# Moving three groups of work and folding one more projection chunk in a one-layer hybrid mixer with a mixture of experts

## The chip, the core and the metric

The kernel runs on one core of one Trainium2 chip. The metric is the device time of one execution in microseconds. The engines of the core are TensorE (PE, with its weight loads as PEld), VectorE (DVE), ScalarE (ACT), GpSimd (POOL) and SyncE (SP); 16 DMA engines move data between DRAM and the on-chip memory. Everything is float32.

## What is computed

272 tokens (16 learned meta tokens and 256 of the sequence) of width 2048 pass one decoder layer. The normalised tokens go through one input projection into 52 tiles of 128 columns; an HGRN, an mLSTM and a Mamba-2 mixer read them; the joined outputs go through an output projection and are added to the residual. A mixture of 32 experts follows (one group, then two experts in it, for each token), with a residual add and a last norm. In short:

```python
h = concat([meta, x])                                   # 272 x 2048
u = rmsnorm(h, norm_mix_w)
proj = u @ w_in                                         # 2048 x ~6.7k
(hq, hf, hi, hg, mq, mk, mv, mo, mi, mf, sz, sxbc, sdt) = split_last(proj, IN_SPLITS)
y_a = hgrn2_mixer(hq, hf, hi, hg, lower_bounds, hg_norm_w)
y_b = mlstm_mixer(mq, mk, mv, mo, mi, mf, ml_b_i, ml_b_f, ml_norm_w)
y_c = mamba2_mixer(sz, sxbc, sdt, conv_w, conv_b, dt_bias, a_log, d, ssm_norm_w)
h = h + concat([y_a, y_b, y_c]) @ w_out                 # 2048 x 2048
h = h + hierarchical_moe(rmsnorm(h, norm_ffn_w), ...)   # 32 experts, 3 matrices of 4 MB each
return rmsnorm(h, final_norm_w)[:, N_META:]

# where it matters below
f = lower_bound + (1 - lower_bound) * sigmoid(hf)       # HGRN's decay; its log is summed over the tokens
y_b = group_rmsnorm(h_ml, norm_w, 4) * sigmoid(mo)      # mo: the last four tiles, MO
y_c = group_rmsnorm(y * silu(z), norm_w, 4)
```

## The kernel before, in words

Each engine has its own instruction stream, written out by hand; the order of the work is the order in those streams, and semaphores tie them together. Nothing is planned by a program.

**Projections.** The input projection is worked through in 26 chunks (c = 0 to 25) of 256 columns, two tiles of 128 columns each (u = 2c and 2c + 1), in the order of `ORDER`: HF, HQ, HV, X0, B0, C0, MQ, MK, MV, HG_, Z0, MO. Chunks 2 and 3 are HQ, chunks 4 and 5 HV, chunk 19 is the second half of HG_, chunks 20 to 23 are Z0, and chunks 24 and 25 the four MO tiles. Eight more chunks (26 to 33) are the output projection. A chunk of weights is 2 MB. SP loads it (L506) into one of two buffers as soon as TensorE has finished the chunk two places before (`in_tile`, L498). ACT takes a finished tile out of PSUM (`tile_out`, L793).

**Folded chunks.** For the chunks in `FOLD` (L228) the product of a chunk is not made as 2 x 16 products over all tokens, but by a seven-product scheme on 2 x 2 blocks: `folded_tiles` makes blocks 0 to 6, each of 8 products over half of the tokens. Blocks 2, 4 and 6 (and 3) need sums and differences of weight blocks, made on POOL by `weight_sums(c)` in four instructions (L643, L645, L646, L650), where block 2 waits for the second, block 3 for the third and block 6 for the fourth. The sums of a folded chunk after the first start when block 4 of the folded chunk before is done (`fold_ps`). The matching sums of token blocks, `uS`, are made once on DVE by `sums_of_tokens` (L1163 to L1168); they are written over hT, the residual, so the residual is first written to DRAM (`h_rows`, L490), and DVE waits for that write (`X_IN[0]`). After the last folded chunk SP loads it back (L500). DVE joins the blocks with `adds_a` and `adds_b` (L1174); block 5 waits for the first of these additions.

**The start.** SP loads the tokens, chunks 0 and 1 and three narrow strips `wg`, and then writes `h_rows` (L489, L490, waiting for ACT's ninth copy `x_ev`). ACT issues ten small parameter loads (L773). TensorE makes the first tiles, the gate products (L1945), then turns the parameters (L1753, waiting for all ten loads), and goes on with tiles 2 to 7.

**HGRN's part around chunk 4.** DVE makes a memset (L1354), the token sums, and then eight scalings (L1358, L1360) which end in the signal `hlin`; ACT makes the logarithm (L882) and only then takes out tiles 6 and 7; DVE scales HQ (L1364), makes four scans (L1368), four differences (L1242, L1243) and then the additions of chunk 4. Block 2 of chunk 4 waits for tile 7's being taken out.

**Mamba's part around chunk 19.** DVE makes for eight pairs of heads the decays (`ssm_decay`, L1291) and the scores (`ssm_scores`, L1302, six instructions, signal `pt_ready`). TensorE's `ssm_pair` (L1911) waits for them. POOL, having spread the last rows, starts the sums of chunk 19 when its weights have landed.

**The end of the mixers.** Chunk 24 is not folded. ACT takes out its tiles with a sigmoid (L942, L945), squares what the norms need and makes the inverse roots (`inverse_rms`); TensorE makes the norms' sums (L1894) behind tiles 49 and 50.

**The experts.** From expert 0 on SP streams the 96 matrices of 4 MB through four buffers, each load released by TensorE's having used the one before it in its buffer.

Of the kernel before, what the change touches and what calls it, by code (L numbers as in the profile page):

```python
# [28 lines left out]
def hymba_moe_layer(nc, x, meta_tokens, hg_lb_logits, norm_mix_w, w_in, hg_norm_w, ml_b_i, ml_b_f,  # L29
# [7 lines left out]
    ACT = mybir.ActivationFunctionType  # L37
# [5 lines left out]
    NM = meta_tokens.shape[0]  # L43
    SEQ = x.shape[1]
    T = NM + SEQ
    KD = D // P
# [4 lines left out]
    HGH, MLH, SSH, SSG = 4, ml_b_i.shape[1], ssm_d.shape[1], 4  # L51
# [47 lines left out]
    with ctx:  # L99
# [17 lines left out]
        def wchunk(j):  # L117
            return slot(j).rearrange("p (k c) -> p k c", k=KD)
# [108 lines left out]
        wT = part(13376, NA * P)  # L227
        FOLD = (4, 5, 11, 12, 13, 19, 20, 21, 22, 23)  # L228
        NF = len(FOLD)
# [241 lines left out]
        def columns(w, c):  # L471
            return w[0, :, bass.ds(c, CH)].rearrange("(k p) c -> p k c", p=P)

        @block.sync
        def _(sp):
# [12 lines left out]

            sp.wait_ge(s["x_ev"], 9)  # L489
            sp.dma_start(h_rows, big[:, RING + KD * T:RING + 2 * KD * T]).then_inc(X_IN[0], 16)  # L490
            for c in range(2, (NIN + NOUT) // 2):
# [6 lines left out]
                sp.wait_ge(s["in_tile"], 2 * c - 2)  # L498
                if c == FOLD[-1] + 2:
                    sp.dma_start(big[:, RING + KD * T:RING + 2 * KD * T], h_rows).then_inc(X_IN[1], 16)  # L500
                w, col = (w_in, COLS[2 * c]) if 2 * c < NIN else (w_out, P * (2 * c - NIN))
                if 2 * c == NIN + NOUT - 2:
                    for h in range(2):
                        sp.dma_start(last_chunk[:, h, :, :], columns(w, col)[:, :, h * P:(h + 1) * P]).then_inc(s["in_b"], 16)
                else:
                    sp.dma_start(wchunk(c % 2), columns(w, col)).then_inc((s["in_a"], s["in_b"])[c % 2], 16)  # L506
                if 2 * c == NIN + 2:
                    sp.wait_ge(s["norm_done"], 1)
                    sp.dma_start(eslot(0), matrix(0, 0)).then_inc(m_in[0], 16)
# [58 lines left out]
        def _(pool):  # L568
# [61 lines left out]
            def weight_blocks(c):  # L630
                w = wchunk(c % 2)
                return [[w[:, 8 * k:8 * (k + 1), j * P:(j + 1) * P] for j in range(2)] for k in range(2)]

            def weight_sums(c):
                n = FOLD.index(c)
                s1, s2, s4 = sums_at(c)
                (b11, b12), (b21, b22) = weight_blocks(c)
                if c == 13:
                    pool.wait_ge(s["ho_ps"], HGH)
                if n:  # L640
                    pool.wait_ge(s["fold_ps"], 5 * n)
# [85 lines left out]
        def _(act):  # L727
# [198 lines left out]
            for u in range(40, 48):  # L926
# [11 lines left out]
                if u == 47:  # L938
                    act.wait_ge(s["in_ev"], 4 + 48)
                    V.activation(proj[:, Z0 + 4:Z0 + 8, :], proj[:, Z0 + 4:Z0 + 8, :], ACT.Silu).then_inc(s["z_gate"], 1)  # L940
                    den_abs(3)
            tile_out(48, ACT.Sigmoid)  # L942
            squares(s["ml_h"], MLH, mlo, sqH)
            act.dma_start(nwc[:, :], norm_ffn_w[0].rearrange("(p c) -> p c", c=KD)).then_inc(s["nw_in"], 16)
            tile_out(49, ACT.Sigmoid)  # L945
            squares(s["ssm_gated"], 1, proj[:, Z0:Z0 + 8, :].rearrange("p (g j) t -> p j g t", j=2),
                    sq8.rearrange("p (j g) t -> p j g t", j=2))
            inverse_rms(1, 1, rs4)
            tile_out(50, ACT.Sigmoid)
            inverse_rms(2, 2, rs4z)  # L950
# [117 lines left out]
        def _(dve):  # L1068
# [389 lines left out]
            for c in range(4, 8):  # L1458
                last = V.tensor_tensor(proj[:, Z0 + c, :], proj[:, Z0 + c, :], proj[:, X0 + c, :], ALU.mult)
            last.then_inc(s["ssm_gated"], 1)  # L1460
            step.link(group_norm(1, mlo, rs4, 4, 1, PL))
            group_norm(2, proj[:, Z0:Z0 + 8, :], rs4z, 4, 2, PS).then_inc(s["z_done"], 1)
            dve.wait_ge(s["in_ev"], 4 + NIN)
            for h in range(MLH):
# [884 lines left out]
```

## Time and profile before

| | |
|---|---|
| median of 3 runs | 1493.99 us (1492.85 to 1494.16) |
| profiled execution | 1492.35 us, of which the span is 1490.4 us |
| PE busy | 1266.8 us (85%) |
| DVE busy | 529.2 us (36%) |
| ACT busy | 279.5 us (19%) |
| POOL busy | 179.6 us (12%) |
| DMA engines, first 14 of 40 slices | 2 to 9 tenths busy |
| DMA engines, last 24 slices | 9 tenths or more, about 430 GB/s |
| PEclk, first 16 slices | 9 tenths or more |
| PEclk, later | 8 or 9 tenths |

The span is cut into 40 slices of 37.3 us. The projections and mixers fill the first 15 of them; the rest is the experts. A time like 339.89 is counted from the start of the span. The page's chain of work that ended last gives PE 52% and DMA 43% of the span.

### The profile page before, as it was taken

The page shows a single profiled execution, that of the slowest core. Times are in us where ns is not written, and L with a number is a line of the kernel's source. Part 1 is how long each engine was busy: PE and PEld are TensorE (multiplying, and loading weights), DVE is VectorE, ACT ScalarE, POOL GpSimd, SP SyncE. Part 2 cuts the span into 40 slices and gives each one's busy share as a digit, 9 for nine tenths or more (in the row PEclk, how much of TensorE's full clock was granted, in tenths as well). Part 3 has the DMA queues.
Part 4 walks back from the last instruction along what each step waited for, and adds up shares of the span by engine and source line. Part 5 has one row for each costly group of instructions (what it writes and reads, how often), then busy time and mean ns, then how long its engine had stood idle before and what let it go on. Part 6 is the DMA issues. An engine that isn't in the chain of part 4 may idle for free.

```text
span 1490.4 us, 20152 instructions
## 1 busy us (share of the span) xinstructions
PE 1266.8 (85%) x8506; PEld 757.1 (51%) x8506; DVE 529.2 (36%) x1177; ACT 279.5 (19%) x423; POOL 179.6 (12%) x144
## 2 busy tenths in 40 slices
PE   8999999999999999876878688778768776787797
PEld 6898899778999995322222232223222322232242
DVE  3543666444624214452232223223322321322234
ACT  3212413112240123111111111111111110000003
POOL 3140043015604730000000000000000000000000
PEclk9999999999999999989898888888898988888898
DMA  9442354444557668999999999999999999999997
GB/s 294 155 151 85 104 141 150 144 135 125 159 173 260 249 206 358 433 429 431 431 430 430 433 432 431 433 432 431 432 433 433 428 432 434 427 431 433 428 432 316
DMA packets 107051, 488.88 MB, mean 328 GB/s; under 512 B 20012, under 2 KB 91976, under 8 KB 93288
## 3 DMA queue, kind: packets, MB, share of 16 engines
q1 hardware_dynamic: 104608, 483.11, 80.5%
q0 software_dynamic: 1104, 3.49, 0.7%
q10 hardware_dynamic: 1272, 1.28, 0.2%
q8 instruction: 54, 0.88, 0.2%
q14 instruction: 13, 0.11, 0.0%
HBM read 483.40 MB, written 4.61 MB: 327 GB/s over the span
## 4 chain that ended last, share of the span: by engine, by line
PE 52%; DMA 43%; DVE 3%; issue 1%; ACT 0%; ACTq 0%; SPq 0%; POOL 0%; DVEq 0%; POOLq 0%
DMA big<-in_moe_w_dram 41%; PE bank L1719 22%; PE bank L2156 8%; PE bank L2078 5%; PE bank L2185 3%; PE bank L2198 3%; PE bank L1832 2%; PE bank L2132 2%; PE bank L2169 2%; PE bank L1869 1%; PE bank L1845 1%; DVE big L1302 1%; PE bank L1911 1%; DMA brow<-in_moe_b_router_dram 1%; DMA out_dram<-big 1%
## 5 line engine op out<-in xcount | busy, mean ns | idle before, releaser
L2156 PE MATMUL bank<-big 128*32 128x512 f32 x2016 | 292.0, 733 | 192.4 <-DMA big<-in_moe_w_dram 191.3
L1719 PE MATMUL bank<-big 128*128 128x272 f32 (+4 forms) x2144 | 365.6, 331 | 2.5 <-ACT big L793 1.3
L1719 PEld LDWEIGHTS bank<-big 128*128 128x128 f32 x2144 | 320.2, 191 | 37.8 <-ACT big L793 1.9
L2156 PEld LDWEIGHTS bank<-big 128*32 128x32 f32 x2016 | 74.2, 131 | 406.3 <-issue 207.3
L1558 DVE COPY big<-bank 128x512 f32<-128x512 f32 x32 | 22.1, 691 | 510.5 <-PE bank L2156 509.7
L1571 DVE TENSOR_TENSOR big<-big,bank 128x512 f32<-128x512 f32 x240 | 146.1, 679 | 12.3 <-PE bank L2198 12.3
L2185 PE MATMUL bank<-big 128*32 128x512 f32 x992 | 127.8, 661 | 0.5 <-DVE big L1563 0.5
L2198 PE MATMUL bank<-big 32*128 32x512 f32 x480 | 127.1, 633 | 0.7 <-ACT big L1020 0.7
L721 POOL DMA_INDIRECT out_dram<-big,mlev x1 | 1.1, 1089 | 812.1 <-DMA out_dram<-big 812.1
L1007 ACT ACTIVATE big<-bank 128x512 f32<-128x512 f32 x32 | 19.1, 597 | 369.8 <-PE bank L2132 369.8
L2198 PEld LDWEIGHTS bank<-big 32*128 32x128 f32 x480 | 46.8, 183 | 61.8 <-DVE big L1571 41.2
L2185 PEld LDWEIGHTS bank<-big 128*32 128x32 f32 x992 | 31.6, 119 | 91.2 <-issue 90.2
L2078 PE MATMUL bank<-big 128*128 128x128 f32 x672 | 76.7, 276 | 0.0
L2078 PEld LDWEIGHTS bank<-big 128*128 128x128 f32 x672 | 75.7, 192 | 0.1
L2169 PEld LDWEIGHTS bank<-selq,big 128*128 128x128 f32 x496 | 57.7, 191 | 26.0 <-issue 26.0
L2132 PE MATMUL bank<-big 128*32 128x512 f32 x512 | 62.3, 607 | 6.6 <-issue 6.6
L1020 ACT ACTIVATE big<-bank 128x512 f32<-128x512 f32 x31 | 18.5, 597 | 252.5 <-PE bank L2185 252.5
L2169 PE MATMUL bank<-selq,big 128*128 128x32 f32 x496 | 61.1, 277 | 0.0
L643 POOL TENSOR_TENSOR big<-big 128x1024 f32<-128x1024 f32 x10 | 24.0, 2401 | 164.6 <-DMA big<-in_w_in_dram 109.6
L1495 DVE TENSOR_TENSOR big<-big,bank 128x256 f32<-128x256 f32 (+1 forms) x54 | 18.4, 360 | 64.2 <-PE bank L2078 64.2
L1011 ACT ACTIVATE big<-bank 128x512 f32<-128x512 f32 x32 | 19.1, 597 | 116.9 <-PE bank L2156 116.9
L793 ACT ACTIVATE big<-bank 128x272 f32<-128x272 f32 (+1 forms) x30 | 12.2, 410 | 150.8 <-PE bank L1719 150.8
(345 smaller groups left out, 1098.2 us busy)
## 6 DMA issues: line engine op xcount, KB each, us to landing
big<-in_moe_w_dram SPq DMA_DIRECT2D x92, 4096.0 KB, 32.7
big<-in_w_in_dram SPq DMA_DIRECT2D x25, 2048.0 KB, 8.3
big<-in_w_out_dram SPq DMA_DIRECT2D x7, 2048.0 KB, 8.4
big<-in_moe_w_dram SPq DMA_DIRECT2D x6, 2048.0 KB, 21.0
big<-in_moe_w_dram SPq DMA_DIRECT2D x4, 1024.0 KB, 20.2
h_rows<-big SPq DMA_DIRECT2D x1, 2176.0 KB, 8.8
big<-gate_rows POOLq DMA_DIRECT2D x8, 272.0 KB, 3.6
big<-h_rows SPq DMA_DIRECT2D x1, 2176.0 KB, 9.0
```

What stands on the lines that cost most here:

```text
L643: V.tensor_tensor(s1, b12, b11, ALU.subtract).then_inc(s["fold_ready"], 1)
L1007: V.activation(xs, pb[0][:, :], ACT.Copy).then_inc(signal("xs_ev", x), 1)
L1558: V.tensor_copy(hs3.rearrange("t (k p) -> t k p", p=P), pb[3][:, :].rearrange("t (p k) -> t k p", k=KF)).then_inc(signal("h3_ev", x), 1)
L1571: V.tensor_tensor(h2[:, a, d * 512:(d + 1) * 512], h2[:, a, d * 512:(d + 1) * 512], pb[SUM_BANKS[j]][:, :], ALU.add).then_inc(signal("y_ac ...
L1719: last = V.matmul(outs, a, b, start=start and j == 0, stop=stop and j == n - 1)
L1832: last = V.matmul(pb[(OUT0 + u % 2) % 4][:, 0:SEQ], w, proj[:, MIXED[k], NM:T], start=k == 0, stop=k == 7)
L2078: last = V.matmul(pb[(7 * n + i + 2 + OUT0) % 4][:, 0:SH], w[:, k, :], m, start=k == 0, stop=k == 7)
L2132: last = V.matmul(pb[0][CAP * g:CAP * (g + 1), :], oh[:, a, :], u2[:, a, g * 512:(g + 1) * 512], start=a == 0, stop=a == NA - 1)
L2156: last = V.matmul(pb[2 + r][CAP * g:CAP * (g + 1), :], xsT[:, k % 4, k // 4, :], w[:, k, :], start=j == 0, stop=j == 3)
L2169: last = V.matmul(pb[4][:, (r * KF + k) * CAP:(r * KF + k + 1) * CAP], hs[:, k * P:(k + 1) * P], selq[:, :], start=True, stop=True)
L2185: last = V.matmul(pb[5][CAP * g:CAP * (g + 1), :], hTb[:, k * CAP:(k + 1) * CAP], w[:, k, g * 512:(g + 1) * 512], start=k == 0, stop=k == ...
L2198: V.matmul(pb[SUM_BANKS[j]][:, :], wT[CAP * g:CAP * (g + 1), a * P:(a + 1) * P], ysb[CAP * g:CAP * (g + 1), :], start=True, stop=True).the ...
```

## The change

There are four parts.

1. The write of the residual to `h_rows` and its wait move from ahead of the loop over the chunks to behind the load of chunk 3.
2. Two waits are added on POOL: the sums of chunk 4 wait for `hlin` (HGRN's eight scalings), and those of chunk 19 for the eighth `pt_ready` (the last scores).
3. Chunk 24 is folded too. TensorE makes it in seven blocks; POOL makes four sums more; DVE's additions for it stand ahead of the group norms; ACT copies its first block, and makes the sigmoid of both tiles in one instruction behind the first inverse roots, and DVE waits for that (`z_gate`). With one folded chunk more, the PSUM banks of the chunks behind it turn by one.
4. The load of the residual back from `h_rows` is issued one chunk later (26 in place of 25), and behind that chunk's weights in place of ahead of them.

```diff
-        FOLD = (4, 5, 11, 12, 13, 19, 20, 21, 22, 23)
+        FOLD = (4, 5, 11, 12, 13, 19, 20, 21, 22, 23, 24)
...
-            sp.wait_ge(s["x_ev"], 9)
-            sp.dma_start(h_rows, big[:, RING + KD * T:RING + 2 * KD * T]).then_inc(X_IN[0], 16)
             for c in range(2, (NIN + NOUT) // 2):
...
                 sp.wait_ge(s["in_tile"], 2 * c - 2)
-                if c == FOLD[-1] + 2:
-                    sp.dma_start(big[:, RING + KD * T:RING + 2 * KD * T], h_rows).then_inc(X_IN[1], 16)
...
                     sp.dma_start(wchunk(c % 2), columns(w, col)).then_inc((s["in_a"], s["in_b"])[c % 2], 16)
+                if c == FOLD[-1] + 2:
+                    sp.dma_start(big[:, RING + KD * T:RING + 2 * KD * T], h_rows).then_inc(X_IN[1], 16)
+                if c == 3:
+                    sp.wait_ge(s["x_ev"], 9)
+                    sp.dma_start(h_rows, big[:, RING + KD * T:RING + 2 * KD * T]).then_inc(X_IN[0], 16)
...
                 (b11, b12), (b21, b22) = weight_blocks(c)
+                if c == 4:
+                    pool.wait_ge(s["hlin"], 1)
                 if c == 13:
                     pool.wait_ge(s["ho_ps"], HGH)
+                if c == 19:
+                    pool.wait_ge(s["pt_ready"], SSH // 2)
...
-            tile_out(48, ACT.Sigmoid)
+            first_product(24)
             squares(s["ml_h"], MLH, mlo, sqH)
             act.dma_start(nwc[:, :], norm_ffn_w[0].rearrange("(p c) -> p c", c=KD)).then_inc(s["nw_in"], 16)
-            tile_out(49, ACT.Sigmoid)
             squares(s["ssm_gated"], 1, proj[:, Z0:Z0 + 8, :].rearrange("p (g j) t -> p j g t", j=2),
                     sq8.rearrange("p (j g) t -> p j g t", j=2))
             inverse_rms(1, 1, rs4)
+            act.wait_ge(s["in_ev"], 4 + 50)
+            V.activation(proj[:, MO:MO + 2, NM:T], proj[:, MO:MO + 2, NM:T], ACT.Sigmoid).then_inc(s["z_gate"], 1)
             tile_out(50, ACT.Sigmoid)
...
             last.then_inc(s["ssm_gated"], 1)
+            adds_a(24)
+            adds_b(24)
             step.link(group_norm(1, mlo, rs4, 4, 1, PL))
             group_norm(2, proj[:, Z0:Z0 + 8, :], rs4z, 4, 2, PS).then_inc(s["z_done"], 1)
+            dve.wait_ge(s["z_gate"], 3)
             dve.wait_ge(s["in_ev"], 4 + NIN)
```

## Rows read from the trace of the kernel before

**Rows 1.** Busy time by stretch: start, length, PE, PEld, DVE, ACT, POOL, PEclk, DMA, GB/s
```profile
620.00:900.00 280.00, 215.65 (x1444) 77.58 (x1448) 85.15 (x194) 43.86 (x57) 3.16 (x10) 0.87 1.00 431
```

**Rows 2.** Waits behind 560: waiting line, what it waited for, total us, times, longest
```profile
PE bank L2156 <- DMA big<-in_moe_w_dram: 191.3, 55, 7.4
```

**Rows 3.** Timeline of SP at 578: start, length, engine, line, operation, tensors, count
```profile
578.00 0.33 SPq L525 DMA_DIRECT2D big<-in_moe_w_dram  x1
```

**Rows 4.** Timeline of PE, start to 90; in brackets the idle time before and its releaser
```profile
32.88 0.33 PE L1753 MATMUL bank<-ident,big 128*128 128x128 f32 x1 [2.41 <-DMA brow<-in_moe_b_router_dram]
...
63.85 17.79 PE L1719 MATMUL bank<-big 128*128 128x256 f32 x96 [0.50 <-DVE colc L1156]
82.95 5.83 PE L1719 MATMUL bank<-big 128*128 128x136 f32 x48 [1.31 <-ACT big L793]
89.34 10.92 PE L1719 MATMUL bank<-big 128*128 128x136 f32 x92 [0.56 <-DVE big L1174]
```

**Rows 5.** Timeline of PE, around the last pair and around chunks 23 and 24
```profile
339.89 1.14 PE L1911 MATMUL bank<-big 128*64 128x272 f32 x12 [2.35 <-DVE big L1302]
...
405.47 12.77 PE L1719 MATMUL bank<-big 128*128 128x128 f32 x112
...
420.41 14.08 PE L1719 MATMUL bank<-big 128*128 128x256 f32 x64
```

**Rows 6.** SP's issues of the residual's write and of chunk 3; the page's DMA issue row
```profile
23.09 0.96 SPq L490 DMA_DIRECT2D h_rows<-big  x1
...
49.03 0.37 SPq L506 DMA_DIRECT2D big<-in_w_in_dram  x1
...
h_rows<-big SPq DMA_DIRECT2D x1, 2176.0 KB, 8.8
```

**Rows 7.** DMA queues (packets, MB, share): SP's q1 and ACT's q10, 26:27; q10, 30:31
```profile
q1 hardware_dynamic: 23, 0.40, 93.4%
q10 hardware_dynamic: 23, 0.00, 1.6%
...
q10 hardware_dynamic: 330, 0.02, 21.4%
```

**Rows 8.** Timeline of DVE, 64 to 89
```profile
64.22 1.50 DVE L1354 MEMSET big<- 128x1728 f32 x1 [0.43 <-DVE colc L1156]
...
71.51 0.41 DVE L1360 TENSOR_SCALAR big<-big,lb 128x272 f32<-128x272 f32 x1
71.84 2.45 DVE L1358 TENSOR_SCALAR big<-big,lb 128x272 f32<-128x272 f32 x1
...
83.21 0.73 DVE L1364 TENSOR_SCALAR big<-big 128x1088 f32<-128x1088 f32 x1 [1.74 <-ACT big L793]
83.85 2.56 DVE L1368 TENSOR_TENSOR_SCAN big<-ones,big 128x272 f32<-128x272 f32 x4
...
89.00 1.50 DVE L1174 TENSOR_TENSOR big<-big,bank 128x136 f32<-128x136 f32 x5
```

**Rows 9.** Timeline of ACT, the logarithm
```profile
81.51 1.11 ACT L882 ACTIVATE big<-big 128x1088 f32<-128x1088 f32 x1 [16.96 <-DVE big L1360]
```

**Rows 10.** Timeline of POOL: first sums of chunks 4, 5, 19 and 23
```profile
71.77 2.36 POOL L643 TENSOR_TENSOR big<-big 128x1024 f32<-128x1024 f32 x1 [10.94 <-DMA big<-in_w_in_dram]
...
88.86 2.44 POOL L643 TENSOR_TENSOR big<-big 128x1024 f32<-128x1024 f32 x1 [7.55 <-PE bank L1719]
...
329.64 2.35 POOL L643 TENSOR_TENSOR big<-big 128x1024 f32<-128x1024 f32 x1 [2.92 <-DMA big<-in_w_in_dram]
...
398.56 2.36 POOL L643 TENSOR_TENSOR big<-big 128x1024 f32<-128x1024 f32 x1 [6.42 <-PE bank L1719]
```

**Rows 11.** Timeline of DVE: scores of pairs 6 and 7; second half of the Z products
```profile
322.72 1.75 DVE L1302 SCALAR_TENSOR_TENSOR big<-big,colc 128x272 f32<-128x272 f32 x6
...
330.89 8.94 DVE L1302 SCALAR_TENSOR_TENSOR big<-big,colc 128x272 f32<-128x272 f32 x6
...
423.74 1.49 DVE L1459 TENSOR_TENSOR big<-big 128x272 f32<-128x272 f32 x4
```

## The prediction

> **What bounds the kernel now.** I read the busy times by stretch first. In the experts' part the DMA engines are busy throughout (1.00, 431 GB/s) while PE is busy 215.65 of 280 us [rows 1], and PE's greatest wait there is for the weights, 191.3 us [rows 2]. So that part lasts as long as its bytes, whatever TensorE does. What matters is when it begins: from 578.00 on every load is released by TensorE's having used a buffer [rows 3], and that moment is the end of the mixers and the output projection, where PE is busy nearly throughout. So the second view is PE's timeline up to there, read for its gaps. A microsecond of PE idle taken away ahead of 578 should start the stream a microsecond earlier and be a microsecond off the end. The gaps that the change can reach are four: 2.41 us ahead of the parameters' transposes, 1.31 and 0.56 us in chunk 4 [rows 4], 2.35 us ahead of the last pair of heads [rows 5]. Besides them it shortens a busy stretch, chunk 24.
>
> **Part 1, the residual's write.** PE waits for the parameters 2.41 us, until 32.88 [rows 4]. SP issued the write of 2.2 MB at 23.09, and it landed 8.8 us later [rows 6], so it was on the way until 31.9. Between 26 and 27 SP's queue moved 23 packets with 0.40 MB, 17 KB each, and ACT's queue, which carries the parameters, moved 23 too, all tiny. The two queues took turns, packet by packet, and a tiny packet waited out a large one each time. Between 30 and 31, when the write was through, ACT's queue moved 330 [rows 7]. Without the write its backlog needs some 2 us: five microseconds at 25 a microsecond and the 330 make about 450 packets, which at 330 a microsecond are gone by about 27. With 2 us for landing that is 29, and PE is ready at 32.88 - 2.41 = 30.47. The gap goes entirely: **-2.4 us**. Bounds: 0 and 2.41, since PE has work right up to it.
> The Trainium skill says the same of the queues (DMA: Bandwidth & Descriptors, Queues, rings and completion order: each DMA engine goes round its queues and changes at packet boundaries). By that rule the write disturbs whoever shares the engines with it, now POOL's loads of the gate rows; what this can do stands in the rivals.
>
> Where does the write go? All times of before up to chunk 4 move 2.4 earlier. Chunk 3 is issued at 49.03 - 2.4 = 46.6 [rows 6]; nothing else of SP waits behind the write for long (chunk 4 is issued when tile 5 is done, some 14 us later; `x_ev` is long there). The 2 MB of chunk 3 go ahead of it at about 0.4 MB a microsecond [rows 7], 5.3 us, then the write's 8.8: it lands at about 61.1 with 1 us for the issues counted in. DVE needs it for the token sums, behind the memset: 64.22 + 1.5 - 2.4 = 63.3 [rows 8]. The slack is 2 us; at the cost of nothing, then, as long as the write takes under 11 us from chunk 3's end.
>
> **Part 2a, the sums of chunk 4.** DVE's scalings took 0.33 us each (71.51 to 71.84) until POOL began at 71.77 [rows 10], then 2.45 [rows 8]: each waited for one POOL instruction. The last four cost 8 us more, the logarithm started at 81.51 [rows 9], and tiles 6 and 7 came out behind it: PE's 1.31 us. DVE came to the additions at 89.00 [rows 8]: PE's 0.56 us. With the wait, DVE makes eight scalings in 8 x 0.33 from 70.5 - 2.4 on: `hlin` at 70.8. POOL's four sums follow, 9.5 us, until 80.4. ACT: logarithm until 72, tile 6, then tile 7 when PE has it. PE: 63.85 + 17.79 - 2.4 = 79.2 is when block 2 is wanted, and the two blocks before it take 5.83 / 3 = 1.94 each, so tile 7 is ready at 75.3 and out at 75.75. The second sum, which block 2 needs, is there at 70.8 + 4.8 = 75.6. So the 1.31 us go. Block 5 is wanted at 79.2 + 5.83 = 85.1, and the first addition must be done. DVE has from the scaling of HQ to the additions 89.00 - 83.21 = 5.8 us of work [rows 8], but now POOL runs beside it from 75.75 to 80.4. The HQ scaling ends with POOL's third instruction, about 78. The scans (two inputs in SBUF) have no row beside POOL. Their price is bounded by 0.65 each (2.56 for four [rows 8]) and by one POOL instruction, 2.4, for each that meets one. I take the dear end, since the scores with the same operand kinds pay it [rows 11]: one scan until 80.5, then three scans and four differences, 4.5 us, additions at 85.0, first one done at 85.3. PE waits 0.2, against 0.56 before; with cheap scans nothing. The gain is 1.87 - 0.2: **-1.7 us**, bounds 1.9 and, by the rival below, -0.8 (a loss).
> The Trainium skill (SBUF — State Buffer, SBUF: two separate sides) has the rule: VectorE and GpSimd share a port pair as an exclusive lock, for a fast-mode VectorE operation or one with two inputs in SBUF. By it the scans are blocked as I took them; were the lock for fast modes alone, the 0.2 us would be nothing. The six scores of part 2b, which have two such inputs, took 8.94 in place of 1.75 us, so the trace agrees.
>
> **Part 2b, the sums of chunk 19.** Pair 6's scores took 1.75 us, pair 7's 8.94 from 330.89 on, while POOL's sums ran from 329.64 [rows 10, 11]; PE waited 2.35 for them [rows 5]. PE wants the scores at 337.5. Uncontended they are done at 332.6, 5 us ahead. POOL starts there, 3 us later than before, and has its second sum at 337.4, its fourth at 342.2. PE makes the pair 337.5 to 338.6 and blocks 0 and 1 until 342.2; block 2 finds its sum 5 us old, block 6, another 7 us on, its own as well. What is queued behind POOL's wait are only these sums; the last row loads stand ahead of it. **-2.35 us**, bounds 2.35 and 2.35 less one POOL instruction.
>
> **Part 3, chunk 24 folded.** Unfolded it takes 14.08 us, folded chunk 23 of the same width 12.77 [rows 5]: **-1.3 us**. Its sums start when block 4 of chunk 23 is done, 405.47 + 5 x 1.8 = 414.6, and end at 424.1; block 2 is wanted at 420.4 + 3.6 = 424.0, block 6 at 431. For chunk 23 POOL began 6.9 us ahead of the chunk [rows 5, 10], here 5.8. DVE's last products were at 423.74 to 425.2 [rows 11]; now one or two of its operations wait for POOL, 2.4 at most beyond 424.1: additions from 426 or 427 on, wanted at 429.5. ACT's one sigmoid over two tiles is bounded by the 1.11 us of an instruction with twice the elements [rows 9], plus a table load, and lies beside tile 50's 7 us. POOL's pair sum of squares waits behind the sums, and has 10 us. Part 4, the residual's load back, leaves with chunk 26's weights: two transfers of 5.3 us from about 433 on, done by 447, and DVE wants it at 464. Neither PE nor the stream sees it. Bounds of part 3: 1.3 and 1.3 - 2.4 (one more blocked operation than the slack holds).
>
> **The sum.** 2.4 + 1.7 + 2.35 + 1.3 = 7.75 us of PE time ahead of 578, all on the path. The profiled execution took 1492.35 (span 1490.4): 1484.6, span 1482.7. Its time lies 1.6 under the median of the runs, 1493.99, whose scatter is 1.3: forecast **1486.3**.
>
> **The rivals.**
> - *One blocked difference in chunk 4.* POOL's sums for chunk 5 start at 85.15, when block 4 is done (88.86 after 88.78 before [rows 4, 10]). DVE's last difference starts at 84.35. If DVE is some 0.8 us later it meets POOL and ends at 87.5: PE waits 2.7 us. The time is 1486.3 + 2.5 = 1488.8. For it: the write shares the engines with some 1.4 MB of gate rows; byte for byte shared, it would land 3 us later, over its slack by 1. Against: [rows 7] show turns by packet, in which 2 KB packets hold up 17 KB ones little. Chance 0.13.
> - *The parameters are no earlier*, because their own issue or latency, not the write, held them: 1488.7. Against it stand the 330 packets of one microsecond [rows 7]. Chance 0.05.
> - *The stream doesn't start earlier* or gives the gain back, being bound by its bytes: 1493.5 or so. Against: up to 578.00 the loads wait for PE [rows 3]. Chance 0.05.
> - *Slower: DVE is caught in POOL's chunk 5 sums altogether.* With five or more two-input operations left at 85.15 it gets one step for each of POOL's four sums and then finishes, 96 us: PE waits 11 us in chunk 4, and 1.87 + 2.4 + 2.35 + 1.3 = 7.9 are not enough: 1493.99 - 7.9 + 11 = 1497.1. It decides from a landing of the write at 66 or later, 5 us beyond my estimate. Chance 0.02.
>
> **How the numbers follow.** Forecast 0.70, the four rivals 0.25, the rest (small shifts of either sign) 0.05. A measurement of this kernel can tell 0.2%, 3 us, from no change. Faster by more: 0.70 + 0.13 + 0.05 and most of the rest, 0.92; same 0.05, slower 0.03. The range takes in the forecast, the first two rivals and the scatter of 0.7 to either side: 1484.5 to 1489.8.
>
> **What would show it.** The row of L1753 has no idle time before it and starts near 30.5. The write is issued near 47 and DVE's token sums start near 63. All eight scalings take 0.41. L643 of chunk 4 follows `hlin`; PE's gap before block 2 is gone, the one before block 5 at most 0.3. The eighth L1302 group takes 1.75, and PE's gap before L1911 is gone. Chunk 24 stands as 112 instructions of 12.8 us. The first buffer's reload, 578.00 before, is at about 570.3. Wrong would be: DVE idle ahead of its token sums for the write, a difference (L1242, L1243) of 2.4 us, or a stream that starts earlier and ends no earlier.

## The result and the profile after

The change makes the kernel **slower**: 1498.44 us (median of 8 runs, 1497.78 to 1499.6) against 1494.0 for the kernel before (median of 8, 1492.85 to 1494.98); the ratio is 1.0021, with a 95% interval of 1.0012 to 1.0031. The forecast was 1486.3, its range 1484.5 to 1489.8. The profiled execution took 1497.94, its span 1496.2.

Three of the four gains did arrive, 6.0 us together, but more is lost at two other places. First TensorE's gaps in the mixers (timeline of PE, kernel after: start, length, line, operation, tensors, count, and in brackets the idle time before and its releaser):

```profile
30.58 0.33 PE L1762 MATMUL bank<-ident,big 128*128 128x128 f32 x1
...
61.56 19.95 PE L1728 MATMUL bank<-big 128*128 128x256 f32 x112 [0.50 <-DVE colc L1162]
82.15 3.94 PE L1728 MATMUL bank<-big 128*128 128x136 f32 x32 [0.64 <-POOL big L651]
95.30 14.89 PE L1728 MATMUL bank<-big 128*128 128x136 f32 x113 [9.20 <-DVE big L1180]
...
336.78 1.14 PE L1920 MATMUL bank<-big 128*64 128x272 f32 x12
...
344.95 1.14 PE L1920 MATMUL bank<-big 128*64 128x272 f32 x12
...
425.49 12.77 PE L1728 MATMUL bank<-big 128*128 128x128 f32 x112
...
455.36 13.98 PE L1841 MATMUL bank<-big 128*128 128x256 f32 x64
```

The parameters' transposes start at 30.58 with no idle time, 2.3 us earlier than before [rows 4]. The last pair has lost its gap [rows 5], and chunk 24 takes 12.77 in place of 14.08. But ahead of block 5 of chunk 4 TensorE now waits 9.20 us, where it waited 0.56. What this does to the lead over the kernel before: chunk 4 begins 2.29 us earlier (61.56 against 63.85), the seventh pair 7.49 later (336.78 against 329.29), the eighth 5.06 later, the output projection's 64 products 3.76 later (455.36 against 451.60). The experts' stream starts as much later (SP, kernel after; against 578.00 in [rows 3]):

```profile
581.77 0.33 SPq L526 DMA_DIRECT2D big<-in_moe_w_dram  x1
```

The engines that feed block 5, DVE first (kernel after):

```profile
63.34 1.23 DVE L1169 TENSOR_TENSOR big<-big 128x1088 f32<-128x1088 f32 x1
...
70.55 0.41 DVE L1366 TENSOR_SCALAR big<-big,lb 128x272 f32<-128x272 f32 x1
76.11 0.94 DVE L1370 TENSOR_SCALAR big<-big 128x1088 f32<-128x1088 f32 x1 [5.16 <-ACT big L798]
76.98 8.96 DVE L1374 TENSOR_TENSOR_SCAN big<-ones,big 128x272 f32<-128x272 f32 x4
85.97 0.73 DVE L1248 TENSOR_TENSOR big<-big 128x544 f32<-128x544 f32 x1
86.61 2.87 DVE L1249 TENSOR_TENSOR big<-big 128x544 f32<-128x544 f32 x1
89.40 2.86 DVE L1248 TENSOR_TENSOR big<-big 128x544 f32<-128x544 f32 x1
92.18 2.86 DVE L1249 TENSOR_TENSOR big<-big 128x544 f32<-128x544 f32 x1
94.96 1.50 DVE L1180 TENSOR_TENSOR big<-big,bank 128x136 f32<-128x136 f32 x5
```

and POOL (kernel after):

```profile
52.80 0.74 POOL L622 DMA_DIRECT2D gate_rows<-gX  x1 [22.92 <-DVE gZ L1159]
...
61.41 0.58 POOL L628 DMA_DIRECT2D big<-gate_rows  x1 [6.84 <-DMA gate_rows<-gZ]
62.22 1.61 POOL L628 DMA_DIRECT2D big<-gate_rows  x3 [0.22 <-issue]
74.12 2.36 POOL L648 TENSOR_TENSOR big<-big 128x1024 f32<-128x1024 f32 x1 [10.28 <-DMA big<-in_w_in_dram]
76.56 2.71 POOL L650 TENSOR_TENSOR big<-big 128x1024 f32<-128x1024 f32 x1
79.23 2.77 POOL L651 TENSOR_TENSOR big<-big 128x1024 f32<-128x1024 f32 x1
81.97 2.77 POOL L655 TENSOR_TENSOR big<-big 128x1024 f32<-128x1024 f32 x1
86.17 2.72 POOL L648 TENSOR_TENSOR big<-big 128x1024 f32<-128x1024 f32 x1 [1.44 <-PE bank L1728]
```

DVE is on time: its token sums start at 63.34, its eight scalings end at 70.96, as forecast. POOL isn't. Its sums start at 74.12, and what released them is **chunk 4's weights**, not `hlin`, 3.2 us earlier. From 76.98 to 84.7 and again from 86.17 on each of DVE's two-input operations then takes as long as a POOL instruction: three of the four scans 2.8 to 2.9 us each, while the fourth, behind POOL's last sum, takes 0.69 (8.96 together, 2.56 before [rows 8]), and three differences 2.9 each in place of 0.72. So the additions stand at 94.96 and not at 85.0.

Why the weights are late stands in the DMA issues (kernel after, the stretches 47 to 50, 50 to 56 and 60 to 61: operation and count, KB each, us from issue to landing):

```profile
h_rows<-big SPq DMA_DIRECT2D x1, 2176.0 KB, 13.8
...
gate_rows<-gX POOLq DMA_DIRECT2D x1, 17.0 KB, 6.7
gate_rows<-gG POOLq DMA_DIRECT2D x1, 4.2 KB, 6.9
gate_rows<-gZ POOLq DMA_DIRECT2D x1, 4.2 KB, 7.1
...
big<-in_w_in_dram SPq DMA_DIRECT2D x1, 2048.0 KB, 13.4
```

The write is issued at 47.15 and lands at 61.0. POOL's three tiny writes of gate rows, issued in that time, took 2.3, 1.9 and 1.8 us before and take 6.7 to 7.1 now. POOL waits for them [6.84 <-DMA gate_rows<-gZ] and reads the rows back at 61.41 instead of 58.43, which is 2.3 us earlier plus a 5.3 us delay. By then chunk 4's load (issued at 60.55) is under way, and the two share the engines: between 66 and 70 POOL's queue moved 0.97 MB and SP's 0.31. Chunk 4's weights take 13.4 us where they took 8.9.

On top of this TensorE's **granted clock** falls (kernel after: start, length, busy time of PE, PEld, DVE, ACT, POOL, then PEclk, DMA share and GB/s):

```profile
88.00:90.00 2.00, 0.00 (x0) 0.00 (x0) 2.00 (x2) 0.00 (x0) 1.92 (x2) 0.56 0.00 0
...
96.00:98.00 2.00, 2.00 (x11) 2.00 (x11) 0.46 (x2) 0.00 (x0) 0.00 (x0) 0.50 0.00 0
98.00:100.00 2.00, 2.00 (x17) 2.00 (x17) 0.30 (x1) 0.00 (x0) 0.00 (x0) 0.88 0.04 8
100.00:102.00 2.00, 2.00 (x19) 2.00 (x19) 0.30 (x1) 0.00 (x0) 1.12 (x1) 1.00 0.09 6
```

0.50 is 1.2 GHz: TensorE makes 11 products in 2 us in place of 19 or 20, until some 3 us after it has work again. From 95.3 on, 2.7 us at 0.50 and 2 at 0.88 cost 1.6 us. The sum up to the seventh pair: 10.06 us of gaps in chunk 4 (9.20, 0.64, and 0.22 within the row of 19.95, whose products took 17.79 and 1.94 before) against 1.87 are 8.2 more, the clock 1.6, the start was 2.3 earlier: 7.5, and 7.49 is read.

The second place is the **tail**. Of the span's 5.8 us more, 3.77 are there at the stream's start and 3.15 at DVE's last instruction; then POOL is another 2.67 late with the last rows of the output. Kernel after:

```profile
1487.16 0.75 DVE L1718 SCALAR_TENSOR_TENSOR big<-big,mlev 128x512 f32<-128x512 f32 x1
1491.87 1.09 POOL L726 DMA_INDIRECT out_dram<-big,mlev  x1 [813.36 <-issue]
```

and kernel before:

```profile
1484.01 0.75 DVE L1709 SCALAR_TENSOR_TENSOR big<-big,mlev 128x512 f32<-128x512 f32 x1
1486.05 1.09 POOL L721 DMA_INDIRECT out_dram<-big,mlev  x1 [812.06 <-DMA out_dram<-big]
```

Before, POOL starts 2.04 us behind the start of DVE's last product, released by an output write; after, 4.71 us behind, and waiting for nothing that the profile shows. In between lies one packet of an instruction queue (q14, between 1489 and 1490); before, it comes only after POOL's write is issued (between 1491 and 1492).

### The profile page after: what moved, and what is told of

It is laid out like the page before. It is cut to its first block, busy times and chain, and to the rows that moved or that the text cites. A ratio compares the mean times of both kernels' runs of the same rounds, so it can differ in the third digit from the quotient of the medians.

```text
span 1496.2 us, 20269 instructions
## 1 busy us (share of the span) xinstructions
PE 1275.5 (85%) x8554; PEld 760.3 (51%) x8554; DVE 529.9 (35%) x1184; ACT 279.0 (19%) x422; POOL 190.7 (13%) x148
## 3 DMA queue, kind: packets, MB, share of 16 engines
q0 software_dynamic: 1104, 3.49, 0.7%
## 4 chain that ended last, share of the span: by engine, by line
PE 56%; DMA 41%; DVE 2%; issue 1%; ACT 0%; SPq 0%; POOL 0%; DVEq 0%; POOLq 0%
DMA big<-in_moe_w_dram 40%; PE bank L1728 24%; PE bank L2165 8%; PE bank L2087 5%; PE bank L2194 4%; PE bank L2207 3%; PE bank L1841 2%; PE bank L2141 2%; PE bank L2178 2%; PE bank L1878 1%; PE bank L1854 1%; DVE big L1374 1%; PE bank L1920 1%; DMA big<-in_x_dram 1%; DMA out_dram<-big 0%
## 5 line engine op out<-in xcount | busy, mean ns | idle before, releaser
L2165 PE MATMUL bank<-big 128*32 128x512 f32 x2016 | 292.9, 735 | 187.7 <-DMA big<-in_moe_w_dram 186.6
L1728 PE MATMUL bank<-big 128*128 128x128 f32 (+4 forms) x2192 | 366.0, 327 | 10.5 <-DVE big L1180 9.2
L2194 PE MATMUL bank<-big 128*32 128x512 f32 x992 | 134.4, 690 | 0.5 <-DVE big L1572 0.5
L2141 PE MATMUL bank<-big 128*32 128x512 f32 x512 | 62.3, 607 | 3.3 <-DVE big L1547 3.3
L2178 PE MATMUL bank<-selq,big 128*128 128x32 f32 x496 | 61.1, 277 | 0.0
L1180 DVE TENSOR_TENSOR big<-big,bank 128x128 f32<-128x128 f32 (+2 forms) x77 | 20.8, 288 | 65.1 <-PE bank L1728 64.7
## 6 DMA issues: line engine op xcount, KB each, us to landing
big<-h_rows SPq DMA_DIRECT2D x1, 2176.0 KB, 14.2
```

What stands on the lines that cost most here:

```text
L1180: return V.tensor_tensor(out_, in_, pb[(START[c] + i) % 4][:, 0:m], ALU.add)
L1728: last = V.matmul(outs, a, b, start=start and j == 0, stop=stop and j == n - 1)
L2141: last = V.matmul(pb[0][CAP * g:CAP * (g + 1), :], oh[:, a, :], u2[:, a, g * 512:(g + 1) * 512], start=a == 0, stop=a == NA - 1)
L2165: last = V.matmul(pb[2 + r][CAP * g:CAP * (g + 1), :], xsT[:, k % 4, k // 4, :], w[:, k, :], start=j == 0, stop=j == 3)
L2178: last = V.matmul(pb[4][:, (r * KF + k) * CAP:(r * KF + k + 1) * CAP], hs[:, k * P:(k + 1) * P], selq[:, :], start=True, stop=True)
L2194: last = V.matmul(pb[5][CAP * g:CAP * (g + 1), :], hTb[:, k * CAP:(k + 1) * CAP], w[:, k, g * 512:(g + 1) * 512], start=k == 0, stop=k == ...
```

## The experiments

**The theory** from these traces: the write behind chunk 3 slows the small writes of gate rows, these put POOL's big reads into chunk 4's load, POOL starts its sums 3 us late, and DVE is caught with its scans in the sums of chunk 4 and with three differences in those of chunk 5. Rivals: the added wait for `hlin` does it; or the write itself, by its place in SP's queue; or the collision of DVE and POOL is no cause but a symptom.

**The write alone** (kernel before with part 1 only).

```diff
-            sp.wait_ge(s["x_ev"], 9)
-            sp.dma_start(h_rows, big[...]).then_inc(X_IN[0], 16)
...
+                if c == 3:
+                    sp.wait_ge(s["x_ev"], 9)
+                    sp.dma_start(h_rows, big[...]).then_inc(X_IN[0], 16)
```

> The kernel before with part 1 alone: the residual's write behind chunk 3, no wait added on POOL, chunk 24 unfolded. Theory (the write's new place): the write holds up POOL's three small row writes, which land near 61; the gate rows then run into chunk 4's load, its weights land near 74, and POOL's sums meet DVE's scans and differences although POOL has no wait. PE then idles about 9 us ahead of block 5 and its clock falls to 0.5 for a few us: 1494 - 2.3 + 8 + 1.5 = 1501 us. Rival (the added wait puts the sums on top of the scans): without that wait the gaps in chunk 4 stay near 2 us: 1491.5 us.

Measured: 1501.91 against 1494.99 on the same chip, ratio 1.0032 (1.0013 to 1.0051). Without any wait for `hlin` POOL's first sum stands where it does in the full change:

```profile
74.12 2.36 POOL L644 TENSOR_TENSOR big<-big 128x1024 f32<-128x1024 f32 x1 [10.50 <-DMA big<-in_w_in_dram]
```

The scans take 8.95, the last three differences 2.87, 2.86 and 2.86, TensorE waits 0.36, 0.64 and 9.20. With the write behind chunk 3 the added wait has no part in the loss of chunk 4; part 1 alone makes it. The loss is greater than the full change's because the gains of parts 2b and 3 are missing, and because in this execution the clock also stood at 0.50 behind the gap of 2.31 us ahead of the last pair: the stream starts at 587.08.

**The wait for `hlin` alone** (kernel before with part 2a only).

```diff
+                if c == 4:
+                    pool.wait_ge(s["hlin"], 1)
```

> The kernel before with the wait of chunk 4's sums on hlin alone. Theory (the write's new place is what hurts): hlin at 73.2, sums 73.2 to 83.5, HQ's scaling at 78.1 and one scan meet them, additions near 88, PE idle 0.5 to 1 us ahead of block 5 in place of 1.87 in two gaps; if the last difference meets chunk 5's sums, 3.5. 1493 us, 1495.5 at the worst. Rival (the wait itself): PE idle some 9 us ahead of block 5, 1501 us.

Measured: 1500.06 against 1494.99, 1.0033 (1.0021 to 1.0044), a miss for both. The sums follow `hlin`, and the scans take 4.72; but the last difference starts at 89.39, POOL's sums for chunk 5 at 89.06: it takes 2.86 us, and TensorE waits 3.54 us, after which the clock stands at 0.50 from 92 to 96. So part 2a costs more than it brings even where the write is at its old place: one gap of 3.54 us and the clock behind it, in place of 1.87 us in two gaps. Not all of the measured loss is its own. The clock fell two more times in this execution, behind gaps that the kernel before has too: the parameters' gap, here 2.75 us (0.76 and 0.50 from 32 to 36), and the last pair's, here 2.40 (0.76 and 0.50 from 346 to 350).

**The write behind chunk 2**, the rest of the change as it is.

```diff
-                if c == 3:
+                if c == 2:
```

> The changed kernel with the residual's write behind the load of chunk 2 in place of chunk 3, where no other transfer runs for some 10 us. Theory: parameters still early (PE gap of 2.4 gone), small row writes land in 2 us, chunk 4's weights near 70, POOL starts at hlin near 71. PE idle ahead of block 5 0.3 to 3: 1486.5 to 1489.5 us. Rival (the wait on hlin): chunk 4 stays as in the changed kernel, 1498 us.

Measured: 1491.46 against 1494.99, 0.9974 (0.9965 to 0.9984): faster than before, 2 us above the range expected. The small writes take 2.3, 1.9 and 2.0 us, chunk 4's load 8.7, and POOL starts behind `hlin` (timeline of POOL):

```profile
70.93 2.36 POOL L648 TENSOR_TENSOR big<-big 128x1024 f32<-128x1024 f32 x1 [12.30 <-DVE big L1366]
...
84.88 2.62 POOL L648 TENSOR_TENSOR big<-big 128x1024 f32<-128x1024 f32 x1 [4.04 <-PE bank L1728]
```

The loss left is the blocked difference, the first rival of the prediction (timelines of DVE and PE):

```profile
85.21 2.87 DVE L1249 TENSOR_TENSOR big<-big 128x544 f32<-128x544 f32 x1
...
88.34 21.99 PE L1728 MATMUL bank<-big 128*128 128x136 f32 x153 [3.54 <-DVE big L1180]
```

and the clock behind it is at 0.50 (busy time by stretch, columns as above):

```profile
90.00:92.00 2.00, 2.00 (x11) 2.00 (x10) 0.00 (x0) 0.00 (x0) 2.00 (x2) 0.50 0.00 0
```

**The write at its old place**, the rest of the change as it is.

```diff
+            sp.wait_ge(s["x_ev"], 9)
+            sp.dma_start(h_rows, big[...]).then_inc(X_IN[0], 16)
             for c in range(2, (NIN + NOUT) // 2):
...
-                if c == 3:
-                    sp.wait_ge(s["x_ev"], 9)
-                    sp.dma_start(h_rows, big[...]).then_inc(X_IN[0], 16)
```

> The changed kernel with the residual's write back at its old place, ahead of the loop. Theory: the parameters' gap of 2.4 us is back, chunk 4 as in the kernel with its wait alone, the pair's gap of 2.35 and 1.3 of chunk 24 are gone: 1489.5 us, up to 1492 if a difference meets chunk 5's sums. Rival (the wait on hlin): 1500 us.

Measured: 1496.56 against 1494.99, 1.0006 (0.9994 to 1.0018): a miss. The gap before block 5 is 3.55 us as in the two runs above, the parameters' gap 2.94, and the clock fell behind both. The stream starts at 580.99, 2.99 us later than before.

**The wait of chunk 19 alone** (kernel before with part 2b only).

```diff
+                if c == 19:
+                    pool.wait_ge(s["pt_ready"], SSH // 2)
```

> The kernel before with the wait of chunk 19's sums on the last scores alone. Theory (scores and sums exclude each other): pair 7's six scores take 1.75 us in place of 8.94, PE's gap of 2.35 ahead of them is gone, no new gap; the experts' first reload comes 2.35 earlier: 2.35 us less than before. Rival (part 2b gives nothing, since PE waits for the later sums instead): a gap of 2 us ahead of block 2 or 6 of chunk 19, same time as before.

Measured: 1490.59 against 1494.33, 0.9981 (0.9970 to 0.9993). The scores take 1.75 us, TensorE has no gap before the last pair. The stream starts at 574.75, 3.25 us earlier; of this some 0.9 is no work of the part, since chunk 4's gaps were 1.00 us in this execution against 1.87.

**Chunk 24's folding alone** (kernel before with parts 3 and 4):

```diff
-        FOLD = (4, 5, 11, 12, 13, 19, 20, 21, 22, 23)
+        FOLD = (4, 5, 11, 12, 13, 19, 20, 21, 22, 23, 24)
```

> The kernel before with parts 3 and 4 alone: chunk 24 folded, the residual's load back one chunk later. Theory: chunk 24 takes 12.8 in place of 14.1 us, no new gap up to 578, the experts' first reload 1.3 earlier: 1.3 us less than before. Rival (the rest of what was lost sits here, in the norms or the later load back): gap of PE between 434 and 470, or no earlier reload; same as before or 1 to 2 us more.

Measured: 1492.9 against 1494.33, 0.9992 (0.9979 to 1.0005), which can't be told from no change. Chunk 24 takes 12.77 us and there is no new gap, but the stream starts at 581.82, 3.8 us later than before, where 1.3 earlier was expected. Two falls of the clock did that, behind gaps which the kernel before has too: the parameters' gap was 2.94 us and the 32 products behind it took 10.53 in place of 7.60, and behind the last pair's gap TensorE makes 14 products in 2 us, where it made 21 at clock 1.00 (timeline of PE, then busy time by stretch):

```profile
343.47 1.80 PE L1915 MATMUL bank<-big 128*64 128x272 f32 x12 [2.31 <-DVE big L1303]
...
344.00:346.00 2.00, 2.00 (x14) 1.37 (x12) 0.50 (x1) 0.00 (x0) 0.00 (x0) 0.50 1.10 376
```

In TensorE's rows both parts do what the prediction says of them; that chunk 24's folding makes the whole kernel faster is not shown by these times.

**POOL's sums of chunk 5 held back** until DVE's differences are done, in the changed kernel, and **the same with the write behind chunk 2**. In the first, only the meeting of the differences with chunk 5's sums is taken away; the late weights and the held scans are left.

```diff
+                if c == 5:
+                    pool.wait_ge(s["lv_d"], 2)
```

> The changed kernel (write behind chunk 3) with POOL's sums of chunk 5 waiting for DVE's fourth difference. Theory: POOL still starts at 74.1 and the scans still take 9 us, but the differences take 0.7 each in place of 2.87, additions at 88.6, PE's gap ahead of block 5 falls from 9.2 to 2.9 us: 1492 us, some 1.5 to 3 more if the clock falls in a gap of this length. Rival (the differences are not held by POOL): gap stays at 9 us, 1498.4 us.

> The changed kernel with the write behind chunk 2, and POOL's sums of chunk 5 waiting for DVE's fourth difference. Theory (the last difference meets chunk 5's sums, and the idle time it makes costs the clock too): that difference takes 0.72 in place of 2.87 us, PE's gap ahead of block 5 falls from 3.5 to about 1.4 us, its clock stays at 1.00: 2.1 + 3 = 5 us less than with the write behind chunk 2 alone, 1486.5 us. Rival (idle time alone is lost, the clock costs nothing): 2.1 us less, 1489.4 us.

Measured: 1491.48 against 1494.87, 0.9972 (0.9958 to 0.9986), for the first, 1487.24 against 1494.33, 0.9956 (0.9943 to 0.9970), for the second. In the first POOL still starts at 74.25 and the scans still take 8.95, but the four differences take 0.72 each, the gap is 2.77 in place of 9.20, and the clock stays at 1.00. The stream starts at 573.92, 7.85 us earlier than in the changed kernel. So this collision is a cause: taking it away gives back 7 us, more than the whole loss. In the second the gap is 1.39 us, and the clock stays at 1.00 too.

**Chunk 4's fourth sum held back** in place of chunk 5's sums, with the write behind chunk 2. Block 6 alone needs that sum, so POOL may leave DVE alone during the scans. Chunk 5's sums follow it in POOL's stream, so they too come behind the differences.

```diff
-                if c == 3:
+                if c == 2:
...
+                if c == 4:
+                    pool.wait_ge(s["lv_d"], 2)
                 V.tensor_tensor(s4, b21, s2, ALU.subtract).then_inc(s["fold_ready"], 1)
```

> The changed kernel with the write behind chunk 2, and the fourth sum of chunk 4 (which only block 6 needs) waiting for DVE's fourth difference. Theory (each scan that meets POOL costs one POOL instruction): HQ's scaling meets the third sum, the scans nothing; additions near 83.5, where block 5 is wanted at 84.8: no gap in chunk 4, clock at 1.00, all that was forecast is there: 1485 us. Rival (block 6 waits for the late sum): a gap of 1 to 2 us one block later, 1487 us.

Measured: **1483.62** (1483.25 to 1484.06) against 1494.33, 0.9932 (0.9918 to 0.9946), the fastest of all. DVE, POOL and PE:

```profile
78.53 2.56 DVE L1376 TENSOR_TENSOR_SCAN big<-ones,big 128x272 f32<-128x272 f32 x4
...
83.83 2.37 POOL L657 TENSOR_TENSOR big<-big 128x1024 f32<-128x1024 f32 x1 [5.81 <-DVE big L1251]
...
61.42 47.36 PE L1730 MATMUL bank<-big 128*128 128x256 f32 x320 [0.50 <-DVE colc L1164]
...
569.43 0.33 SPq L526 DMA_DIRECT2D big<-in_moe_w_dram  x1
```

TensorE has no gap from the start of chunk 4 on through chunk 5, and the stream starts 8.57 us earlier than before.

**The clock's price.** Kernel: the write behind chunk 2, and in the gap before block 5 seven products of no use, so that TensorE isn't idle there.

```diff
+                    if c == 4:
+                        for _ in range(7):
+                            V.matmul(pb[7][:, 0:T], ones[:, 0:P], ones[:, :], start=True, stop=True)
```

> The changed kernel with the write behind chunk 2, and seven products of no use (ones by ones, into a free bank) on PE where it else idles 3.5 us ahead of block 5 of chunk 4. Theory (idle time lets the clock fall to 0.50 for six us, which costs 3 us of products): the products take 3.3 us, the granted clock stays at 1.00 from 84 to 96, block 5 starts at the same 88.3, and the time is 3 us less than with the write behind chunk 2 alone, 1488.5 us. Rival (the fall of the clock has another cause or costs nothing): 1491.5 us or more.

Measured: 1489.85 against 1494.87, 0.9964 (0.9951 to 0.9977). Block 5 starts at the same time, 88.29 in place of 88.34, but at clock 1.00:

```profile
90.00:92.00 2.00, 2.00 (x20) 2.00 (x19) 0.30 (x1) 0.00 (x0) 2.00 (x2) 1.00 0.00 0
```

The seventh pair starts at 328.24 against 331.27, and the stream 3.0 us earlier (573.23 against 576.25). So in these two executions the lower clock costs another 3.0 us behind a gap of 3.5. The medians differ by 1.6 only (1489.85 against 1491.46), where 3.0 was expected; the profiled execution without the filling, 1492.57, is the slowest of its ten (1490.05 to 1492.57), and whether the clock fell in the others isn't known. The Trainium skill says that TensorE falls to its lower clock behind idle time (TensorE: Matmul & The Clock Gate, Part 1). The traces agree in kind, but the length of the gap alone doesn't decide: of the parameters' gaps those of 2.75 and 2.94 us were followed by 0.50 and those of 2.41 and 2.72 were not; ahead of the last pair 2.31 and 2.40 were, 2.35 in the kernel before was not; ahead of block 5 every gap of 3.5 us or more was, and 2.77 was not.

**The gate rows read later**: the changed kernel, with POOL's four row reads placed behind chunk 4's sums.

```diff
+            weight_sums(4)
             for p in range(SSH // 2):
...
-                        if c <= 15:
+                        if 4 < c <= 15:
```

> The changed kernel (write behind chunk 3) with POOL's spreading of the first gate rows behind its sums of chunk 4. Theory (the write holds up the small row writes, so the gate rows' loads run into chunk 4's): chunk 4's load lands in 9 in place of 13.4 us, POOL starts at hlin near 71 in place of 74.1, chunk 4 then goes as with the write behind chunk 2, gap 3.5 us: 1491.5 us. Rival (the write itself delays chunk 4's load, being ahead of it in SP's queue): POOL starts near 74, gap 9 us, 1498 us.

Measured: 1491.57 against 1494.87, 0.9966 (0.9951 to 0.9980), as with the write behind chunk 2, and with a gap of 3.80 us before block 5. The write is still behind chunk 3 and the three small writes still take 6.8 to 7.0 us, but chunk 4's load takes 8.3, and POOL's first sum is released by `hlin`:

```profile
71.24 2.36 POOL L648 TENSOR_TENSOR big<-big 128x1024 f32<-128x1024 f32 x1 [16.88 <-DVE big L1367]
```

The weights were late because of the row reads, then, not because of the write's place in SP's queue.

**POOL's stream made longer**: the changed kernel with 40 tiny memsets in POOL's idle time near 678 us.

```diff
+        pads = sb("pads", [P, 40])
...
+            for i in range(40):
+                V.memset(pads[:, i:i + 1], 0.0)
```

> The changed kernel, and 40 more tiny memsets on POOL right behind its iota near 678 us, where POOL then stands idle for 813 us. They change nothing before that and move POOL's last instructions 40 places further on in its stream. What is asked: of the changed kernel's 1498.4, about 2.7 us lie in the tail: from the start of DVE's last multiplication to POOL's output write it is 4.7 us in its profile against 2.0 in that of the kernel before, with one packet of the instruction queue q14 in between. Theory: that is POOL fetching its own last instructions late, because the change made its stream longer, and where a fetch falls depends on the place in the stream; then with the 40 pads the packet leaves that stretch, the distance is 2.0 to 3.5 us, and the time is 1495.7 to 1497. Rival: the fetch has nothing to do with the place of POOL's instructions (another engine's, or a matter of when the experts' part begins): the packet and 4.4 to 5.8 us stay, and the time is 1498 to 1499. Nothing else changes by either: chunk 4's gap of 9.2 us and the reload at 581.8 stay.

Measured: 1496.66 against 1493.68, 1.0018 (1.0009 to 1.0027). Chunk 4's gap is 9.20 and the reload at 581.39, but the packet of q14 has left the tail, and POOL is on time:

```profile
1487.33 0.75 DVE L1721 SCALAR_TENSOR_TENSOR big<-big,mlev 128x512 f32<-128x512 f32 x1
...
1489.52 1.09 POOL L729 DMA_INDIRECT out_dram<-big,mlev  x1 [810.41 <-DMA out_dram<-big]
```

More instructions make the tail of the profile shorter by 2.5 us (2.19 in place of 4.71). By the medians the loss against the kernel before falls from 4.4 to 3.0 us, but the intervals of the two ratios overlap, so that this difference is less sure. The same distance in the other traces fits: 2.04, 2.22 and 2.04 us with the write alone, the wait for `hlin` alone and the wait of chunk 19 alone, 3.49 with chunk 24's folding alone, and 3.3 to 5.8 in the seven other variants of the changed kernel, six of them with the packet in that stretch. So where the packet falls depends on the place of POOL's instructions in its stream, and the reading that it is a fetch of them fits; in the changed kernel it falls on the last write. Why the distance is 3.3 and 3.5 us in two kernels without such a packet in it stays open.

## Why the prediction was wrong

**What held.** The bound: each kernel's stream starts as much earlier or later as TensorE does, and its end follows within 3 us. Part 1's own gain, 2.4 forecast and 2.3 measured. The write's landing: 61.1 forecast, 61.0 measured (two errors of some 3 us cancel: chunk 3 took 8.7 us in place of 5.3, and the write was then through within 6, not 8.8), and DVE's token sums at 63.34 for 63.3. `hlin` at 70.96 for 70.8. Part 2b: 2.35 forecast, the gap gone and 2.43 between the seventh and eighth pairs' leads. Part 3: 1.3 for 1.3 on TensorE. Part 4: the load back took 14.2 us in place of the two transfers' 10.6, and nobody waited.

**The step that failed** is the one that begins "Where does the write go?" and ends "at the cost of nothing". It asked who waits for the write, and whether others delay it, but not whom the write delays at its new place, though [rows 7] had just shown that at the old one: tiny packets that each wait out a 17 KB one. The same rows were there in the new place: POOL's three small writes at 55.1 before, 2.3 us earlier now, in the middle of the write. The text says that the write disturbs POOL's loads of the gate rows and leaves what this can do to the rivals; the rivals then price it only by a later landing of the write. The Trainium skill's rule of the turns by packet (DMA: Bandwidth & Descriptors, Queues, rings and completion order) was cited on the right side and applied to one queue only. The trace agrees with it in part: from 57 to 60 SP's queue moved 71 packets and POOL's 76. But POOL's first packet moves some 4.6 us behind the first issue (57.4 and 52.80), where it was 1.4 before, and turns by packet don't explain that wait; what held it stays open. That the write is what makes the difference is shown all the same, by 2.3, 1.9 and 2.0 us with the write behind chunk 2.

**The term for part 2a** was wrong in three ways that add up. POOL's start was put at `hlin`, 70.8, and was 74.12, by the weights. One scan was taken as blocked and three as free; the row that was missing is now there: a scan that meets POOL pays one POOL instruction, 2.8 to 2.9 us, three of the four did, and the fourth, at 0.69, paid nothing (8.96 together). And the stretch from the scans to the additions was counted as if POOL were done with chunk 4 at 80.4 and not yet in chunk 5; it was done at 84.7, and three differences paid 2.9 us each from 86.6 on. Where POOL does start at `hlin`, with the write behind chunk 2, one scan is held as forecast (4.72 for the four), and the sum is still wrong, but by little: the last difference starts at 85.21 and POOL at 84.88. The forecast had 84.35 and 85.15 for these; its margin of 0.8 us was given a chance of 0.13 to fail, which was far too low for a difference between two such long sums.

**The rival that came true** is the slower one: DVE caught by POOL's sums for chunk 5, TensorE waiting 11 us for it, 1497.1. Its mechanism was right, and its wait of 11 us about right (9.84 us in two gaps). That its time comes so near 1498.44 is luck in part: it has neither the 1.6 us of the clock nor the 2.67 of the tail, and the medians are 4.4 us apart where the profiled spans are 5.8. Its trigger was wrong: "from a landing of the write at 66 or later". The write landed at 61.0, and what decides is POOL's start, which depends on its weights and they on the gate rows. The chance of 0.02 hung on that trigger.

**What stood in no term**: the granted clock. The rivals price idle time at its length, and a gap of 3.5 us cost 6.5 in all in the profiled execution. And the tail: four sums more for chunk 24 and the waits put POOL's last fetch of instructions ahead of the last write.

The sum in the profile's own terms, to the start of the stream: -2.3 (parameters) + 8.2 (chunk 4's gaps) + 1.6 (clock) - 2.4 (last pair) - 1.3 (chunk 24) = +3.8, and 3.77 is measured. In the experts' part the stream gives back 0.6, and the tail adds 2.67: +5.8 of span. Why the stream gives back 0.6 stays open; from its start to DVE's last product it takes 904.4 to 906.3 us in the runs here.

## What to carry to other kernels

When a transfer is moved, list for its new stretch every other queue with a packet in it, the smallest first, and follow each to who waits for it: a 4 KB write was the link between a 2 MB write and a gap of 9 us, and of two places for the write, one chunk apart, one made the kernel slower and the other faster. Where two engines exclude each other, put a wait on the one whose result is wanted last (chunk 4's fourth sum) rather than hope that a margin of 0.8 us holds. And price a gap on TensorE with the spell of the lower clock as a possible addition: here it came behind gaps from 2.31 us on, in some executions and not in others, and behind every one of 3.5 us or more. Closing such a gap takes the risk away too.

## What the runs showed of the hardware

- Each scan with two inputs in SBUF pays one POOL instruction when both run: 2.8 to 2.9 us in place of 0.64 (three of the four that take 8.96). The Trainium skill has this as an exclusive lock (SBUF — State Buffer, SBUF: two separate sides), and the trace agrees. It works in both directions: POOL's sums beside the scans take 2.71 to 2.77 us in place of 2.36. The scaling of HQ, with one input, is held as well (2.62 us in place of 0.73, with the write behind chunk 2). DVE's additions, which read one input from PSUM, keep their 0.30 us beside POOL (1.50 for five from 89.00 on in the kernel before, with a POOL sum from 88.86 to 91.30 [rows 8, 10]).
- A gap of 3.5 us on TensorE cost 3.0 more by the clock in the profiled execution, one of 9.2 only 1.6, since most of the low spell lies in the gap itself.
- Each gap seems to cost a refill too: in the fastest version chunk 4 starts 2.43 us earlier than before and chunk 5 ends 4.84 earlier, 2.41 more, where the two gaps closed had 1.87 us of idle time: 0.27 a gap beyond it. No run isolates this.
- An engine that has been idle for 812 us can meet a fetch of its own instructions on the last dependence of the program: 2.5 us, removed by 40 instructions of no use (4.71 and 2.19 us from DVE's last product to POOL's write).
